# Other idle products at the head of a two-layer trunk: f32r, 512 to 128 columns wide, in place of 18 fp32 products of 128 columns

## The reference

```python
def reference(x, p, w_in, ...):
    for i in range(DEPTH):                      # DEPTH = 2
        x = x + 0.5 * swiglu(rmsnorm(x, norm_ff1[i]), ff1_w_gate[i], ff1_w_up[i], ff1_w_down[i])
        x = x + token_mixer(rmsnorm(x, norm_mix[i]), w_in[i], ...)
        x = x + 0.5 * swiglu(rmsnorm(x, norm_ff2[i]), ff2_w_gate[i], ff2_w_up[i], ff2_w_down[i])
        g = jax.nn.sigmoid(rmsnorm(x, norm_ple[i]) @ ple_w_gate[i])
        x = x + g * (p[i] @ ple_w_proj[i])
    return rmsnorm(x, norm_final)
```

## Time and profile before

| what | value |
|---|---|
| device time, median of 3 runs | 1180.99 us (1180.85 to 1181.42) |
| the profiled execution: its span | 1179.5 us |
| TensorE busy | 1168.9 us (99%) |
| VectorE busy | 814.0 us (69%) |
| ScalarE busy | 593.7 us (50%) |
| GpSimd busy | 122.8 us (10%) |

### The profile page before, as it was taken

How to read it: one execution, slowest core, us unless ns; L and a number is a source line. 1 busy time by engine, 2 the same in 40 slices (tenths; PEclk the granted TensorE clock), 3 DMA queues, 4 the chain that set the end, 5 groups by cost and what they waited for, 6 DMA issues and landing times.

```text
span 1179.5 us, 24037 instructions
## 1 busy us (share of the span) xinstructions
PE 1168.9 (99%) x10534; PEld 1144.7 (97%) x10534; DVE 814.0 (69%) x939; ACT 593.7 (50%) x669; POOL 122.8 (10%) x136
## 2 busy tenths in 40 slices
PE   9999999999999999999999999999999999999997
PEld 9999999999999999999999999999899999999996
DVE  5866555688978766655786665558798777666455
ACT  5544445555745544444554444447367455444443
POOL 2000001011512000001210000100133020000011
PEclk9999999999999999999999999999999999999998
DMA  7655555545445555555555555554635365555541
GB/s 288 235 203 188 193 201 177 184 156 202 145 149 207 190 188 206 183 204 187 179 202 194 194 199 184 197 203 139 214 140 169 118 235 203 184 204 186 186 172 36
DMA packets 33384, 218.87 MB, mean 186 GB/s; under 512 B 5184, under 2 KB 6016, under 8 KB 7296
## 3 DMA queue, kind: packets, MB, share of 16 engines
q1 hardware_dynamic: 33280, 217.34, 53.2%
HBM read 216.15 MB, written 1.05 MB: 184 GB/s over the span
## 4 chain that ended last, share of the span: by engine, by line
PE 98%; DVE 1%; DMA 1%; ACT 0%; issue 0%; POOL 0%; SPq 0%; POOLq 0%; DVEq 0%
PE psum L385 31%; PE psum L387 31%; PE psum L386 31%; PE psum L665 1%; PE psum L644 1%; DMA x_all<-in_x 1%; PE psum L517 0%; PE psum L578 0%; PE psum L628 0%; PE psum L699 0%; PE psum L424 0%; PE psum L710 0%; PE psum L613 0%; DVE gates L1671 0%; PE psum L733 0%
## 5 line engine op out<-in xcount | busy, mean ns | idle before, releaser
L1222 DVE TENSOR_TENSOR w_lo<-raw,w_hi 128x2048 fp32r<-128x2048 f32 x200 | 457.9, 2293 | 213.5 <-ACT w_hi L856 213.4
L856 ACT ACTIVATE w_hi<-raw 128x2048 fp32r<-128x2048 f32 x201 | 385.2, 1917 | 366.6 <-PE psum L387 360.8
L385 PE MATMUL psum<-hA_hi,w_hi 128*128 128x256 f32 x1360 | 377.9, 278 | 0.0
L386 PE MATMUL psum<-hA_hi,w_lo 128*128 128x256 f32 x1360 | 375.7, 276 | 0.0
L387 PE MATMUL psum<-hA_lo,w_hi 128*128 128x256 f32 x1360 | 375.7, 276 | 0.0
L385 PEld LDWEIGHTS psum<-hA_hi,w_hi 128*128 128x128 f32 x1360 | 255.4, 188 | 2.7 <-issue 2.7
L386 PEld LDWEIGHTS psum<-hA_hi,w_lo 128*128 128x128 f32 x1360 | 255.4, 188 | 0.0
L387 PEld LDWEIGHTS psum<-hA_lo,w_hi 128*128 128x128 f32 x1360 | 255.3, 188 | 0.0
L385 PE MATMUL psum<-hB_hi,w_hi 128*128 128x256 f32 x832 | 230.3, 277 | 1.1 <-DVE w_lo L1654 1.1
L386 PE MATMUL psum<-hB_hi,w_lo 128*128 128x256 f32 x832 | 229.7, 276 | 0.0
L387 PE MATMUL psum<-hB_lo,w_hi 128*128 128x256 f32 x832 | 229.7, 276 | 0.0
(11 more groups left out here) (182 smaller groups left out, 1226.0 us busy)
## 6 DMA issues: line engine op xcount, KB each, us to landing
raw<-in_weights SPq DMA_DIRECT2D x203, 1024.0 KB, 4.9
raw<-in_weights SPq DMA_DIRECT2D x2, 512.0 KB, 6.2
out<-gates SPq DMA_DIRECT2D x3, 256.0 KB, 2.2
x_all<-in_x SPq DMA_DIRECT2D x1, 520.0 KB, 3.9
x_all<-in_x SPq DMA_DIRECT2D x1, 512.0 KB, 6.2
relu<-in_p SPq DMA_DIRECT2D x2, 256.0 KB, 5.0
consts<-in_consts SPq DMA_DIRECT2D x1, 384.0 KB, 5.7
out<-gates SPq DMA_DIRECT2D x2, 128.0 KB, 2.3
```

Source lines behind the costliest of these rows:

```text
L385: pe.matmul(o, lh, rh, start=start, stop=False)
L386: pe.matmul(o, ll, rh, start=False, stop=False)
L856: act.activation(w_hi[:, s, :], raw[:, s, :], ACT.Copy).then_inc(hi_ready[s], 1)
L1222: dve.tensor_tensor(w_lo[:, s, :], raw[:, s, :], w_hi[:, s, :].bitcast(F32), ALU.subtract).then_inc(lo_ready[s], 1)
```

## The change

TensorE now waits for a second semaphore, `warm_ready`, which DVE raises after a memset of 128 x 2048 words in `hid[0]`; the memset stands ahead of all of DVE's other work. The 18 fp32 products are replaced by 26 products in f32r: eight of 512 columns, five pairs of 512 and 256, four of 512 and four of 128. They read both of their operands from `hid[0]`. `as_hi`, `as_lo` and `stream` lie at words 1104, 1648 and 0 of it. The words hold 1.0. The products still write to bank 7, and nothing reads them.

```diff
-WARM = 18
+COLD = 8
...
+        warm_ready = sem("warm_ready")
...
             pe.wait_ge(ones_ready, 1)
-            for _ in range(WARM):
-                pe.matmul(bank[7][:, 0:P], ones[:, :], ones[:, :], start=True, stop=True)
+            pe.wait_ge(warm_ready, 1)
+            flat_ones = hid[0][:, :, :].rearrange("p k t -> p (k t)")
+            stream = flat_ones[:, 0:512]
+            as_hi, as_lo = flat_ones[:, 1104:1232], flat_ones[:, 1648:1776]
+
+            def idle_product(held, columns):
+
+                pe.matmul(bank[7][:, 0:columns], held, stream[:, 0:columns], start=True, stop=True)
+
+            for _ in range(COLD):
+                idle_product(as_hi, 512)
+            for _ in range(5):
+                idle_product(as_hi, 512)
+                idle_product(as_lo, 256)
+            for _ in range(4):
+                idle_product(as_hi, 512)
+            for _ in range(4):
+                idle_product(as_hi, 128)
...
             start_counts(dve, lo_ready)
+            dve.memset(hid[0][:, 0:8, :].bitcast(F32), 1.0).then_inc(warm_ready, 1)
```

## The result

| | us |
|---|---|
| before, median of 21 runs | 1181.37 (1180.85 to 1181.87) |
| changed, median of 21 runs | 1182.55 |
| ratio | 1.0014, 95% interval 1.0008 to 1.0021 |
| profiled execution, span: before, changed | 1179.5, 1180.6 |

The change costs 1.2 us by the medians, against a forecast of 1182.6: slower beyond the interval, but within the 0.2% that the prediction called the same. The times of the changed kernel stand in two groups, eleven from 1182.20 to 1182.55 and nine from 1183.66 to 1183.88; before, they make one spread. One disturbed execution, 4044 us at a mean granted clock of 0.281, is left out of these ranges. So the median is the upper end of the lower group.

What follows compares the result with a forecast made beforehand. TensorE's products were taken to bound the kernel, busy 1168.9 of 1179.5 us. Span 1179.5 + 1.3 (later FFN) + 0.3 (later clock rise) = 1181.1, plus 1.5 around it gives 1182.6 us; range 1180.6 to 1184.4.

Steps and rivals of the forecast that it cites:

- The 1.5 us around the span: Whole run: time that the runs hold around the profiled span, added to 1181.1 to give 1182.6 us.
- What bounds the kernel: Whole kernel: TensorE busy 1168.9 of 1179.5 us; a head edit counts only through FFN start and product pace.
- The memset: DVE at the head: starts near 1.1, takes 2.19 us (1.21 at the lower price); first idle product near 3.3.
- The idle products: TensorE at the head: eight products 0.43 apart, 3.4 us, then 3.06; together 6.5 us against 5.9 before.
- The sum: Head: 3.3 + 6.5 = 9.8 us for the FFN's start; 24 products end at 12.5 instead of 11.20, +1.3.
- The sign that the last product would be late by the FFN's delay less 0.4: Last 256-column product: its start late by the same amount as the FFN's start less 0.4 us.
- The later rise: TensorE's clock at the head: 0.3 us added for a rise later than in one lucky profile.
- half a us for each us: Head: each us of clock rise beyond 3.5 after the first product costs about half a us; c = 5 gives +2.0.
- The tail: Final product pair: clock falls ahead of or behind it; +-0.6 us in the range, nothing in the sum.
- Idle products under cover: Rival at the head: cheap memset (1.2 us) and early rise, +0.3 or less, 1181.0 us; chance 0.22.
- The late rise: Rival at the head: 1.2 GHz for longer than 5.7 us after 3.3; 1183.4 to 1184.5 us; chance 0.20.
- Both changes of pace: Rivals, whole kernel: 113.3 ns product distance improves, about 1168 us (chance 0.07), or worsens, some 1234 us (chance 0.03).

Runs made afterwards that it cites:

- the repetitions: The changed kernel unchanged, three more times: eleven timed runs, eight 1182.24 to 1182.47 and three 1183.58 to 1183.77 us (ratio 1.0011); single executions 1182.22 and 1182.58.
- the short memset with 18 products: Changed kernel with a memset of 512 words instead of 2048 and without its last two loops, 18 f32r products left: 1181.34 us, ratio 1.0000.
- the short memset: Changed kernel with a memset of 512 words instead of 2048, held operands in the first 256 words: 1182.09 us, ratio 1.0005.

## Why the prediction was right, point by point

**The number.** That 1182.6 met 1182.55 so closely is luck in three places. The cost was forecast at 1.6 us (1.3 and 0.3) and is 1.2 by the medians, 1.1 by the spans. The 1.5 us around the span, 1180.99 less 1179.5, set the median of three runs against the span of another execution; wherever a time and its own span are both on record, the distance is 1.8 (1182.38 and 1180.6). With 1.8 the same sum gives 1182.9. And the median lies in the lower group by eleven runs to nine.

**What bounds the kernel.** Right: no wait but those of head and tail, and the pace of 113.3 ns in both kernels. The delay of the head passed to the end, less what was taken back on the way.

**The memset.** Two errors that cancelled. It was put at 1.1 us with a duration of 2.19; it began at 1.49 and took 1.76. From 512 to 2048 words it grew from 0.48 to 1.76 us, 0.83 ns a word, between the two bounds (0.55 and 1.05) and nearer to the dearer one. The Trainium skill ("VectorE: DVE Perf Modes", section "Zero memsets can be issued as uint32 (trn2)") has one element per cycle. By the clock of 0.96 GHz on the same page that is an estimate of 1.04 ns, and the measurement is 20% below it; so the measurement decides. The idle products began at 3.40 for a forecast 3.3.

**The idle products.** 6.5 us forecast, 6.58 measured, in a profile whose clock rose about as early as before's. The pace at the lower level is that of the sum: from two products to five the stretch grows by 1.28 us, 0.43 for each.

```profile
3.97 1.05 PE L830 MATMUL psum<-hid_hi 128*128 128x512 f32 x2
...
3.97 2.33 PE L830 MATMUL psum<-hid_hi 128*128 128x512 f32 x5
```

**The sum.** 9.8 forecast for the FFN's start, 9.98 measured; 12.5 forecast for its 25th product, 12.79 measured. Of the 1.59 us there 0.29 were taken back later, 0.15 of it in the first twelve products behind the third quarter, where the kernel before ran slowly after its wait (the thirteenth begins at 12.71 there and at 14.15 now, 1.44 later). The sum had no term for that. At the end it is 1.22 against a forecast of 1.3, and by the medians 1.2. So here too two errors cancelled: the delay at the 25th product was 0.3 larger than forecast, and 0.37 of it had come back by the last product of 256 columns. The sign that the last product would be late by the FFN's delay less 0.4 was off for the same reason; it is less 0.75.

**The later rise.** 0.3 us were added for it. It exists, and in the repetitions it spans 0.9 us of the FFN's start; but at the end of the lower group it is nearly paid back by the tail, 0.4 of the 0.9 being left. So the term was right in kind, but its size was not borne out. The bound of "half a us for each us" holds at the head alone.

**The tail.** The +-0.6 were right as a bound for the pair (1.22 to 0.70 is 0.5), but not as something independent of the head: the rise and the fall move together. The third group of sums, another 0.4, was not foreseen. If the argument above holds, that is why the upper group at 1183.8 exists: 2.3 to 2.5 us over the median of before in nine of 21 runs, at the edge of the 0.2%, though the changed kernel's median is not.

**The rivals.** Idle products under cover: refuted for the change, and brought about by the short memset with 18 products. The late rise: a rise that comes late is real (up to 5.3 us after the first product, with the short memset), but the 5.7 at which this rival was to decide was seen in no profile. Nine runs lie in the range that it gave, 1183.4 to 1184.5, probably with the tail's help; had two of the other eleven been among them, it would have had the median. Both changes of pace: refuted.

## What to carry to other kernels

Warm-up products have to end before the first real operand is there; whatever feeds them must be ready first, and a 2048-word memset on the way to them (3.4 us until the first product, against 1.2 with a 128-word one) uses up slack that no care in their form won back here. Size the sequence by its longest execution, not by the one in the profile: here the same 26 products took 6.3 to 7.2 us, and 7.4 with the short memset. Read a delay at the end of the program, not where it arises: 0.75 us of it was gone by then. Set a profile beside a median only after asking which of the runs it belongs to. And where times form two groups, look at both ends of the program before looking for two causes.

## What the runs showed of the hardware

- The rise comes after TensorE's own activity, not by itself: 3.5 us after the first product in the run with no idle products, whose FFN started cold. In the other profiles the pace changes between 2.8 us after the first product (the execution with its FFN at 9.72) and 5.3 (the short memset).
- Rise and fall are tied: in four executions of one kernel a later FFN start (9.72, 9.98, 10.25, 10.62) goes with a later fall (1173.6, 1174.1, 1174.8, 1175.6) and a shorter final pair (1.22, 1.12, 0.84, 0.70).
- A DVE memset of float32 grows by 0.83 ns a word here, less than the two-source split (1.05).
- The idle f32r products of 512 columns stand about 0.23 us apart at 2.4 GHz, as real ones do, and 0.43 at 1.2 GHz, and what stands in the head had no effect on the pace behind it (twelve products of 256 columns in 1.36 us in both kernels).
